# GpSimd instead of VectorE for twelve places of low parts of the mixers' weights

## What is computed

```
for l in 0, 1:                                   # first block
    x += 0.5 * swiglu(rms_norm(x), w_gate, w_up, w_down)          # 1024 -> 2816 -> 1024
    proj = rms_norm(x) @ w_in[l]                                  # -> 2464 columns
    y = concat(retention(q, k, v, g), latent_attention(c_q, c_kv, k_rope))
    x += y @ w_o[l]
    x += 0.5 * swiglu(rms_norm(x), ...)
proj = rms_norm(x) @ w_in_2                      # second block, -> 5376 columns
x += (sigmoid(a) * (attention @ w_a) + sigmoid(b) * (two-way gated recurrence @ w_h)) @ w_out
x += mixture of 32 experts, 2 for each token (rms_norm(x))
```

## Time and profile before

| | |
|---|---|
| median of 3 runs | 1783.94 us (1783.86 to 1784.62) |
| profiled execution, its own time | 1780.57 us |
| its span, first to last instruction | 1778.8 us |
| TensorE busy | 1538.4 us, 86% |
| VectorE busy | 945.3 us, 53% |
| ScalarE busy | 633.7 us, 36% |
| GpSimd busy | 58.5 us, 3% |
| low parts (L1128) | 396 instructions, 449.5 us |
| DMA | 407.85 MB, 229 GB/s in the mean |

### The profile page before, as it was taken

The page is one execution under the profiler, slowest core; times in us unless marked ns, Lnnn a source line. Parts: engine busy times, 40 slices in busy tenths (PEclk is TensorE's granted clock), DMA queues, the critical chain, the costliest instruction groups (busy, mean ns, idle before and its releaser), DMA issues.

```text
span 1778.8 us, 30446 instructions
## 1 busy us (share of the span) xinstructions
PE 1538.4 (86%) x12249; PEld 1257.9 (71%) x12250; DVE 945.3 (53%) x1717; ACT 633.7 (36%) x1026; POOL 58.5 (3%) x71
## 2 busy tenths in 40 slices
PE   7999997999999999997999997996859666666666
PEld 7999886799989999885899986885744333333233
DVE  5666686466566666775665667764643222222222
ACT  5444564444444444563544457434310000000000
POOL 1000020000000000010200000000000000000000
PEclk9999998999999999998999998998979988888888
DMA  9555362265565554550555543442099999999996
GB/s 310 188 188 186 127 223 83 72 213 172 188 200 159 193 184 165 169 184 26 184 189 183 189 165 101 134 151 77 15 418 393 430 430 431 431 430 432 434 428 297
DMA packets 147225, 407.85 MB, mean 229 GB/s; under 512 B 5216, under 2 KB 98768, under 8 KB 138976
## 3 DMA queue, kind: packets, MB, share of 16 engines
q1 hardware_dynamic: 145888, 404.31, 61.3%
q0 software_dynamic: 1280, 2.75, 0.7%
HBM read 406.00 MB, written 1.05 MB: 229 GB/s over the span
## 4 chain that ended last, share of the span: by engine, by line
PE 60%; DMA 19%; DVE 9%; issue 5%; ACT 5%; POOL 1%; SPq 0%; POOLq 0%; DVEq 0%; ACTq 0%
DMA expert_gu<-in_exp_gu 19%; PE bank L1869 17%; PE bank L1870 17%; PE bank L1871 17%; PE bank L2448 4%; DVE wlo L1128 2%; ACT whi L702 2%; POOL small L627 1%; ACT prob L811 1%; PE bank L2464 1%; PE bank L2203 1%; DVE x L1185 1%; PE bank L2411 1%; ACT xn L716 1%; ACT hhi L710 0%
## 5 line engine op out<-in xcount | busy, mean ns | idle before, releaser
L1128 DVE TENSOR_TENSOR wlo<-raw,whi 128x1024 fp32r<-128x1024 f32 (+1 forms) x396 | 449.5, 1183 | 150.6 <-ACT whi L702 149.8
L1869 PE MATMUL bank<-hhi,whi 128*128 128x256 f32 x1504 | 427.7, 284 | 8.7 <-DVE hlo L1166 4.3
L1870 PE MATMUL bank<-hlo,whi 128*128 128x256 f32 x1504 | 426.6, 284 | 0.0
L1871 PE MATMUL bank<-hhi,wlo 128*128 128x256 f32 x1504 | 426.6, 284 | 0.0
L702 ACT ACTIVATE whi<-raw 128x1024 fp32r<-128x1024 f32 (+1 forms) x396 | 382.3, 1019 | 92.6 <-PE bank L1871 92.5
L1869 PEld LDWEIGHTS bank<-hhi,whi 128*128 128x128 f32 x1504 | 289.4, 192 | 13.0 <-issue 5.2
L1870 PEld LDWEIGHTS bank<-hlo,whi 128*128 128x128 f32 x1504 | 289.6, 193 | 3.1
L1871 PEld LDWEIGHTS bank<-hhi,wlo 128*128 128x128 f32 x1504 | 289.5, 192 | 0.0
L2448 PE MATMUL bank<-expert_gu,h_e 128*32 128x256 f32 x2112 | 169.9, 492 | 130.6 <-DMA expert_gu<-in_exp_gu 126.4
L2448 PEld LDWEIGHTS bank<-expert_gu,h_e 128*32 128x32 f32 x2112 | 84.6, 140 | 215.8 <-issue 194.4
L1817 DVE SCALAR_TENSOR_TENSOR e_sg<-e_th,bank 128x128 f32<-128x128 f32 x33 | 9.5, 287 | 305.2 <-ACT e_th L1084 305.2
(11 more groups left out here) (358 smaller groups left out, 1652.2 us busy)
## 6 DMA issues: line engine op xcount, KB each, us to landing
expert_gu<-in_exp_gu SPq DMA_DIRECT2D x32, 4096.0 KB, 37.9
expert_dn<-in_exp_dn SPq DMA_DIRECT2D x32, 2048.0 KB, 38.7
raw<-in_ffn_w_gate SPq DMA_DIRECT2D x44, 1024.0 KB, 5.5
raw<-in_ffn_w_up SPq DMA_DIRECT2D x44, 1024.0 KB, 7.4
raw<-in_ffn_w_down SPq DMA_DIRECT2D x44, 1024.0 KB, 4.9
raw<-in_w_in SPq DMA_DIRECT2D x36, 1024.0 KB, 5.1
raw<-in_w_o SPq DMA_DIRECT2D x8, 1024.0 KB, 5.3
raw<-in_w_out SPq DMA_DIRECT2D x4, 1024.0 KB, 5.2
```

The costliest lines, as they stand in the source:

```text
L1128: nc.vector.tensor_tensor(slot_view(wlo, slot, src), src, slot_view(whi, slot, src).bitcast(F32), ALU.subtract).then_inc(lo_ready, inc)
L1869: nc.tensor.matmul(o, sh, mh, start=first, stop=False, skip_group_check=shared)
L1870: nc.tensor.matmul(o, sh, ml, start=False, stop=False, skip_group_check=shared)
L1871: return nc.tensor.matmul(o, sl, mh, start=False, stop=last, skip_group_check=shared)
```

## The change

The low parts of 12 places are formed by GpSimd: places 13, 19, 21 and 23 of a first-kind mixer, and 8, 10, 13, 15, 17, 19, 22 and 24 of the last mixer. The first-kind mixer runs twice, so 16 instructions move. GpSimd's instruction has the same operands and waits for the same count of high parts. In a first-kind mixer GpSimd forms place 13 between its root of 6 columns and its three powers, and 19, 21 and 23 between these and the root of the retention output; in the last mixer all eight stand between its two roots.

GpSimd counts them in a semaphore of its own, `pool_lo_ready`. TensorE waits for that count where it needs such a place. VectorE's count `lo_ready` passes a moved place together with VectorE's next low part, which adds 2. SyncE waits for both counts before it loads over a job. To have the new semaphore, four of the router's semaphores become two that count further; this changes no order.

In the diff, `landed_parts` is what SyncE calls in place of its wait for `lo_ready`, `low_parts` is GpSimd's, the two lines with `continue` are in VectorE's `splits`, and `low_part` is what TensorE calls in place of its wait for `lo_ready`.

```diff
+        POOLED = {"mid": (13, 19, 21, 23), "mix2": (8, 10, 13, 15, 17, 19, 22, 24)}
+        pooled = [m + o for st, _, m in plan if st[0] != "ffn" for o in POOLED[st[0]]]
+        def pooled_below(value):
+            return sum(pos < value for pos in pooled)
...
+            def landed_parts(value):
+                sp.wait_ge(lo_ready, value)
+                if isinstance(value, int) and pooled_below(value):
+                    sp.wait_ge(pool_lo_ready, pooled_below(value))
...
+            def low_parts(i, orders):
+                st, b, m = plan[i]
+                for o in orders:
+                    job, half, _ = mid_order(i, o)
+                    gp.wait_ge(hi_ready, m + o + 1)
+                    src = landed_view((b + job // 3) % 2, st, job, half)
+                    nc.gpsimd.tensor_tensor(slot_view(wlo, m + o, src), src, slot_view(whi, m + o, src).bitcast(F32),
+                                            ALU.subtract).then_inc(pool_lo_ready, 1)
...
                     rsqrt(T, nr[:, 0, :])
+                    low_parts(i, POOLED["mix2"])
                     rsqrt(T * GH)
...
                     rsqrt(6)
+                    low_parts(i, POOLED["mid"][:1])
                     rsqrt(16, r[:, 16:32], 16)
...
+                    low_parts(i, POOLED["mid"][1:])
                     rsqrt(T * RH, r[:, 48:48 + T * RH], 48)
...
+                        if m + o in pooled:
+                            continue
                         if not (nxt and tail):
                             inc = 3 if tail and (job, half) == (3 * batches(i) - 1, 0) else 1
-                            split_lo(plan[i + 1][0] if nxt else st, bb % 2, job, half, m + o, m + o, inc)
+                            split_lo(plan[i + 1][0] if nxt else st, bb % 2, job, half, m + o, m + o, inc + (m + o - 1 in pooled))
...
+            def low_part(pos):
+                if pos in pooled:
+                    pe.wait_ge(pool_lo_ready, pooled.index(pos) + 1)
+                else:
+                    pe.wait_ge(lo_ready, pos + 1)
```

More of the change, by code:

```diff
@@ L247, in program @@
         lo_ready = sem("lo_ready")
+        pool_lo_ready = sem("pool_lo_ready")
         split_used = sem("split_used")
@@ L365, in program @@
         logits_done = sem("logits_done")
-        glogits_ready = sem("glogits_ready")
-        gexp_ready = sem("gexp_ready")
-        elogits_ready = sem("elogits_ready")
-        eexp_ready = sem("eexp_ready")
+        expin_ready = sem("expin_ready")
+        expout_ready = sem("expout_ready")
         picks_ready = sem("picks_ready")
@@ L540, in ffn_batch @@
                     if wait is not None:
-                        sp.wait_ge(lo_ready, wait[j])
+                        landed_parts(wait[j])
                     if j < 2:
@@ L597, in _ @@
                         for w in last_use(last, batches(last) - 2 + k):
-                            sp.wait_ge(lo_ready, w)
+                            landed_parts(w)
                 expert(0, 0, None)
@@ L1071, in experts @@
                                          TR[g][:].rearrange("p (k c) -> p k c", c=P), ACT.Copy).then_inc(hhi_ready, 1)
-                act.wait_ge(glogits_ready, 1)
-                nc.scalar.activation(g4[:, :, 1, :], g4[:, :, 0, :], ACT.Exp).then_inc(gexp_ready, 1)
-                act.wait_ge(elogits_ready, 1)
-                nc.scalar.activation(x8[:, :, 1, :], x8[:, :, 0, :], ACT.Exp).then_inc(eexp_ready, 1)
+                act.wait_ge(expin_ready, 1)
+                nc.scalar.activation(g4[:, :, 1, :], g4[:, :, 0, :], ACT.Exp).then_inc(expout_ready, 1)
+                act.wait_ge(expin_ready, 2)
+                nc.scalar.activation(x8[:, :, 1, :], x8[:, :, 0, :], ACT.Exp).then_inc(expout_ready, 1)
                 act.wait_ge(rows_done, 1)
@@ L1730, in experts @@
                 link(V.tensor_reduce(value(0), gl, AX, ALU.max))
-                V.tensor_tensor(g4[:, :, 0, :], gl, value(0).broadcast_to([P, T, NG]), ALU.subtract).then_inc(glogits_ready, 1)
-                dve.wait_ge(gexp_ready, 1)
+                V.tensor_tensor(g4[:, :, 0, :], gl, value(0).broadcast_to([P, T, NG]), ALU.subtract).then_inc(expin_ready, 1)
+                dve.wait_ge(expout_ready, 1)
                 ge, gh, gt = (g4[:, :, o, :] for o in (1, 2, 3))
@@ L1749, in experts @@
                 V.tensor_tensor(x8[:, :, 0, :], x8[:, :, 5, :], value(4).broadcast_to([P, T, EG]),
-                                ALU.subtract).then_inc(elogits_ready, 1)
-                dve.wait_ge(eexp_ready, 1)
+                                ALU.subtract).then_inc(expin_ready, 1)
+                dve.wait_ge(expout_ready, 2)
                 ee, h1, h2, tm = (x8[:, :, o, :] for o in (1, 2, 3, 4))
@@ L1949, in split_parts @@
                     mm = mid_pos(i, job, half)
-                    pe.wait_ge(lo_ready, mm + 1)
+                    low_part(mm)
                     return [w[:, mm % SLOTS, 0:2 * n].rearrange("p (k n) -> p k n", n=n) for w in (whi, wlo)]
```

## The result

The changed kernel takes 1806.9 us (median of 4 runs, 1806.3 to 1808.2), the kernel before 1783.9 us in the same rounds (4 runs, 1781.0 to 1784.6): a ratio of 1.013, 95% interval 1.012 to 1.015. It is 23.0 us slower, where 16.6 us were forecast; 1806.9 us lies 0.9 us above the upper end of the range. The direction and the charge that it rests on were right, the size was not.

What follows compares the result with a forecast made beforehand. TensorE, busy 86%, was taken as the bound, VectorE counting only where TensorE waits. Last mixer 9.4 us plus first-kind mixers 7.2 gave 16.6 on 1783.94: 1800.5 us, own range 1794 to 1806, reaching down to 1780.0 with the interleaved case.

Steps and rivals of the forecast that it cites:

- the charge: Where VectorE has two-input work queued, GpSimd's reading of 1024 columns holds it off for 2.1 us per moved part.
- The interleaved rival: Long GpSimd reads let VectorE in between elements; no lasting cost, the 3.1 us gain stands: 1780.8 us; chance 0.22.
- the half charge: Rival: GpSimd leaves the read interface after 1.0 us instead of 2.1; 5.5 us in sum, 1789.4 us; chance 0.15.
- The 2.4 us that I took from the words of the Trainium skill: Upper bound of the charge: the read interface is held for GpSimd's full instruction; the sum some 2 us larger.
- What it gives back: Low parts removed from VectorE where TensorE waits: 1.1 us in the last mixer, 1.0 in each first-kind mixer, 3.1 at most.
- The bookkeeping at nothing: Later low-part counts give job buffers back up to 8 us later; loads have cover enough, so costed at nothing.
- Last mixer: Charges of 4.2 and 4.2 us before the scores, less 1.1, plus 2.1 us at place 23's wait: 9.4 us.
- My sentence on place 8: Last mixer: TensorE, waiting 1.3 us for place 8, gets it early and then waits longer for g_kh.
- their three terms: Each first-kind mixer: 2.1 us at rope's last step, 3.1 together with place 16, 0.5 at place 17; 3.6 us, twice 7.2.
- TensorE's clock: Products behind TensorE's lengthened waits: the forecast had no term for a lower granted clock there.

Runs made afterwards that it cites:

- the runs with 32, 512 and 1024: Changed kernel with GpSimd forming only the first 32 or 512 columns of each moved low part, and unaltered with 1024: 1780.2, 1793.4 and 1806.9 us.
- the reading taken away: Changed kernel with GpSimd forming only the first 32 columns of each of its 16 low parts, semaphores and order kept: 1780.2 us, ratio 0.998.
- the half-width run: Changed kernel with GpSimd forming only the first 512 columns of each moved low part: 1793.4 us, ratio 1.006.
- the stall without GpSimd: Kernel before, plus two additional VectorE products of 1024 columns ahead of rope's last step in both first-kind mixers, no GpSimd low part: 1791.2 us, ratio 1.005.
- last mixer only: Changed kernel with only the last mixer's eight places moved to GpSimd, first-kind mixers as before: 1795.9 us, ratio 1.0065.

## Why the prediction was wrong in size

**The charge (right).** 2.1 us a part was read from pairs of 32 and 64 columns and stretched sixteenfold; 1024 columns charge 2.0 to 2.2 us, and the runs with 32, 512 and 1024 lie on one line. The interleaved rival and the half charge fall with it. The 2.4 us that I took from the words of the Trainium skill (SBUF — State Buffer; the words quoted stand in its list of terms) are 0.2 to 0.4 us too long. GpSimd's low part takes 2.35 to 2.40 us alone, of 2.4 forecast.

**What it gives back (right in sum, by luck in its parts).** 3.1 us at most; 3.3 us measured with the reading taken away. But the last mixer gave 2.5 us and not 1.1, and the first-kind mixers 0.3 and 0.1 and not 1.0 each: their wait for place 16 shrank by 0.5 us only, and rope's wait and the part further on took 0.2 and 0.4 of it back.

**The bookkeeping at nothing (right),** by the same run.

**Last mixer (right, with a wait in another place).** Scores 7.1 us later of 7.3; place 23's wait 2.15 us longer of 2.1. My sentence on place 8 (TensorE gets it early and then waits longer for g_kh) missed that the next low part is VectorE's; that moved 3.4 us from one wait into another, with 2.0 us of slower products between the two, and changed no sum.

**First-kind mixers (right in their three terms).** Rope's wait 2.18 us longer of 2.1, place 16's 1.0 longer of 1.0, place 17 0.6 of 0.5 (the starts of TensorE's next products against the mixer's start). One step inside was missed: I had the third power ready at 251.1. GpSimd's powers themselves wait behind VectorE's low parts (6.58 us for two instead of 5.82, and 3.57 for the third), so it came at 252.5; place 16 was late by that much more, and TensorE, at half clock, by as much too, so its wait came out as forecast. The two belong together: in the half-width run the powers are stretched in the mixer with the slower products and not in the other.

**TensorE's clock (the step that failed).** Each term of the sum was a longer wait, and I costed the work behind it at the pace of before: a term of nothing, without a reason given. The row that could have told me is the granted clock by stretches: behind before's longest wait in a first-kind mixer it is 0.57.

```profile
299.11:303.70 4.59, 4.06 (x11) 3.28 (x12) 0.42 (x1) 0.00 (x0) 0.00 (x0) 0.57 0.01 4
```

I didn't look at it for the waits that I forecast to grow. The sizes: 1.5 us behind rope's wait in each of two mixers and 1.6 us behind place 23, 4.6 of the 6.4 us by which the sum fell short. That the first two belong to the longer wait is shown by the stall without GpSimd and by the table, and that they are paid almost in full here (1.4 of 1.5 us), since place 16 comes later with them, by the two mixers of the half-width run. The one behind place 23 is the same reading: of the eleven profiled kernels that leave that place where it is, nine wait 1.5 to 2.5 us there and take 12.5 us for the 60 products, and the two that wait 3.6 us (the changed kernel and last mixer only) take 14.1. No run lengthened that wait without GpSimd. Further on in the two mixers, behind their longest waits, the changed kernel loses another 1.0 and 1.6 us against the profile of before. Unchanged mixers of other runs lose 0.6 us there in the mean, so some 1.2 of these 2.6 us are a fortunate profile of before; the other 1.4 us, and the 0.4 still missing to 23.0, stay open.

**The range.** Its top was the 2.4 us charge, an uncertainty in a term I had. It held nothing for a term I lacked.

## What to carry over

Moving reading work to GpSimd costs VectorE what GpSimd reads, about twice what VectorE would need for it, wherever two-input work is queued there; look for the stretches where VectorE idles, and put it there or nowhere. Before work is moved off an in-order engine, look at what that engine waits for in its list: a low part that stands 6 us too early costs more than its own 1.1 us, and a later place in the same list is the cheaper cure. When a forecast lengthens TensorE's waits, add the slower clock behind them: here 1.5 us for each wait that grew to some 4 us, and in two of four cases at 2.6 to 2.8. Then look for the next wait: where TensorE has to wait there in any case, it takes the loss back (0.2 us left of 1.5 in a mixer without moved parts, nothing left of 2.0 before the scores).

## What the runs showed of the hardware

A GpSimd copy with one SBUF input holds off VectorE's two-input instruction as a subtraction does (0.84 us for 1024 columns, which take 1.04 us). It is not only tensor-tensor work that waits: the small product L1411, one tensor of 16 columns and a constant, 0.18 us before, takes 2.34 us beside a low part:

```profile
252.46 2.37 POOL L647 TENSOR_TENSOR wlo<-raw,whi 128x1024 fp32r<-128x1024 f32 x1
252.53 2.34 DVE L1411 TENSOR_SCALAR small<-small 128x16 f32<-128x16 f32 x1 [0.43 <-POOL small L701]
```

Rope's products, whose main operand is in PSUM, aren't held off; the next one from SBUF is:

```profile
263.63 0.74 DVE L1283 SCALAR_TENSOR_TENSOR rows<-bank,nr,cos_r 128x512 f32<-128x512 f32 x1
264.30 0.74 DVE L1284 SCALAR_TENSOR_TENSOR tmp<-bank,nr,sin_r 128x512 f32<-128x512 f32 x1
265.07 1.25 DVE L1288 TENSOR_TENSOR rows<-rows,tmp 128x256 f32<-128x256 f32 x1
```

with GpSimd's part lying over all three:

```profile
263.63 2.40 POOL L647 TENSOR_TENSOR wlo<-raw,whi 128x1024 fp32r<-128x1024 f32 x1 [5.39 <-ACT whi L726]
```

The Trainium skill (SBUF — State Buffer, Who interferes with whom) draws the line in the same place: two SBUF inputs on VectorE against any GpSimd instruction that reads SBUF, VectorE's scalar products and copies in their faster modes too, and nothing with at most one SBUF input otherwise; the trace agrees, with 2.18 us on L1289, 2.16 on L1411 (whose mode it does not show) and nothing on L1283. And the experts' stage, untouched in every kernel here, comes out at some 471.7 us or at 473.7 to 474.7: a difference of 2.8 us between two profiles is no evidence unless the stage is named in which it lies.
